# A two-layer transformer trunk in fp32r halves: plain weight units of the down projections rounded two at a time

## The reference, cut to what matters

```python
def conv_glu_ffn(h, w_up, conv_w, conv_b, w_down):
    gu = h @ w_up
    gate, up = jnp.split(gu, 2, axis=-1)
    gate = causal_depthwise_conv(gate, conv_w, conv_b)
    return (jax.nn.silu(gate) * up) @ w_down
...
        h = rms_norm(x, ffn_norm[i])
        x = x + conv_glu_ffn(h, ffn_w_up[i], ffn_conv_w[i], ffn_conv_b[i], ffn_w_down[i])
```

## Time and profile before

| | us |
|---|---|
| median of 3 runs | 2084.29 (2084.14 to 2085.8) |
| profiled execution | 2084.77 |
| its span, first to last instruction | 2083.0 |
| TensorE matmul busy | 2072.6 |
| VectorE busy | 1472.6 |
| ScalarE busy | 1069.4 |

### The profile page before, as it was taken

One profiled execution on the slowest core, in us unless ns is written; L12 is line 12 of the kernel. 1 busy time (PEld: TensorE's weight loads), 2 busy tenths in 40 slices (PEclk: granted clock), 3 DMA queues, 4 the chain that ended last, 5 costly groups with the idle time before them and its releaser, 6 DMA issues.

```text
span 2083.0 us, 30160 instructions
## 1 busy us (share of the span) xinstructions
PE 2072.6 (100%) x10836; PEld 1771.6 (85%) x10836; DVE 1472.6 (71%) x1794; ACT 1069.4 (51%) x1379; POOL 0.7 (0%) x5
## 2 busy tenths in 40 slices
PE   9999999999999999999999999999999999999999
PEld 8888888888888888888888877888888888887887
DVE  5655565567767767788986677566767767778887
ACT  6545555544444544455555566554444444445553
POOL 0000000000000000000000000000000000000000
PEclk9999999999999999999999999999999999999999
DMA  7655555656566556578776544566656666668776
GB/s 251 213 176 169 168 175 175 188 172 208 195 201 206 193 195 217 189 231 256 245 252 185 178 147 133 177 188 192 195 190 219 192 198 205 203 201 258 245 257 208
DMA packets 214043, 419.02 MB, mean 201 GB/s; under 512 B 13724, under 2 KB 18636, under 8 KB 213964
## 3 DMA queue, kind: packets, MB, share of 16 engines
q1 hardware_dynamic: 211660, 415.76, 63.3%
q10 hardware_dynamic: 2304, 2.20, 0.3%
HBM read 405.31 MB, written 12.60 MB: 201 GB/s over the span
## 4 chain that ended last, share of the span: by engine, by line
PE 94%; DVE 3%; DMA 1%; ACT 1%; issue 1%; DVEq 0%; ACTq 0%
PE ps L1341 37%; PE ps L1331 31%; PE ps L1337 16%; PE ps L1356 2%; PE ps L1358 2%; PE ps L1357 2%; DMA raw<-in_ffn_w_down 1%; PE ps L1480 1%; DVE wlo L987 0%; PE ps L1537 0%; PE ps L1548 0%; PE ps L1564 0%; PE ps L1581 0%; PE ps L1588 0%; ACT whi L696 0%
## 5 line engine op out<-in xcount | busy, mean ns | idle before, releaser
L1331 PE MATMUL ps<-hs,whi 128*128 128x512 f32 x2832 | 663.6, 390 | 0.0
L1331 PEld LDWEIGHTS ps<-hs,whi 128*128 128x128 f32 x2832 | 524.6, 188 | 104.3
L1034 DVE TENSOR_TENSOR wlo<-raw,whi 128x1024 fp32r<-128x1024 f32 x352 | 418.0, 1221 | 254.9 <-PE ps L1337 222.8
L987 DVE TENSOR_TENSOR wlo<-raw,whi 128x1024 fp32r<-128x1024 f32 x342 | 413.6, 1222 | 218.2 <-ACT whi L696 217.7
L696 ACT ACTIVATE whi<-raw 128x1024 fp32r<-128x1024 f32 x344 | 363.1, 1059 | 347.2 <-PE ps L1341 285.1
L703 ACT ACTIVATE whi<-raw 128x1024 fp32r<-128x1024 f32 x352 | 365.9, 1056 | 262.8 <-DMA raw<-in_ffn_w_up 196.9
L1337 PEld LDWEIGHTS ps<-hs,wlo 128*128 128x128 f32 x2816 | 352.6, 191 | 8.7
L1337 PE MATMUL ps<-hs,wlo 128*128 128x256 f32 x2816 | 355.3, 283 | 0.0
L1341 PE MATMUL ps<-whi,hs 128*128 128x512 f32 x1088 | 275.2, 395 | 0.7 <-ACT whi L696 0.7
L1341 PEld LDWEIGHTS ps<-whi,hs 128*128 128x128 f32 x1088 | 201.2, 188 | 41.7 <-DVE hs L1056 0.9
L1341 PE MATMUL ps<-whi,gs 128*128 128x512 f32 x864 | 214.2, 389 | 0.0
(11 more groups left out here) (190 smaller groups left out, 1559.7 us busy)
## 6 DMA issues: line engine op xcount, KB each, us to landing
raw<-in_ffn_w_up SPq DMA_DIRECT2D x352, 512.0 KB, 4.2
raw<-in_ffn_w_down SPq DMA_DIRECT2D x176, 512.0 KB, 5.2
raw<-in_fox_w_in SPq DMA_DIRECT2D x98, 512.0 KB, 3.9
raw<-in_swa_w_in SPq DMA_DIRECT2D x40, 512.0 KB, 3.7
xs<-mix SPq DMA_DIRECT2D x34, 512.0 KB, 6.0
raw<-in_fox_w_out SPq DMA_DIRECT2D x32, 512.0 KB, 3.7
raw<-in_swa_w_out SPq DMA_DIRECT2D x32, 512.0 KB, 3.7
mix<-mix_out SPq DMA_DIRECT2D x20, 512.0 KB, 6.2
```

What stands on the lines that cost most here:

```text
L987: tt(wlo[slot][:, :], raw[slot][:, :], whi[slot][:, :].bitcast(F32), ALU.subtract).then_inc(lo_ready, 1)
L1034: tt(wlo[slot][:, :], raw[slot][:, :], whi[slot][:, :].bitcast(F32), ALU.subtract).then_inc(lo_ready, 1)
L1331: return pe.matmul(ps[:, bank, :], whi[slot][:, c:c + P], moving.rearrange("p h t -> p (h t)"), start=first, stop=last)
```

## The change

Plain down units from the fifth on (place `RAW` and above in the order) are prepared in twos. At the first of two, ScalarE only waits for its landing and VectorE does nothing. At the second, ScalarE waits for that landing and for `unit_done` of the unit four before the second, and rounds both slots with one operation of 2048 columns, raising `hi_ready` by two; VectorE then makes both remainders with one operation and raises `lo_ready` by two. The buffers of `whi` and `wlo` become one tensor each, so that two neighbouring slots can be named together. SP's code, TensorE's code and the s and t units are unchanged.

```diff
-        whi = [sb(f"whi{s}", [P, UNIT], F32R) for s in range(RAW)]
-        wlo = [sb(f"wlo{s}", [P, UNIT], F32R) for s in range(RAW)]
+        whi_all = sb("whi", [P, RAW, UNIT], F32R)
+        wlo_all = sb("wlo", [P, RAW, UNIT], F32R)
+        whi = [whi_all[:, s, :] for s in range(RAW)]
+        wlo = [wlo_all[:, s, :] for s in range(RAW)]
...
+        def plain_place(u):
+
+            for layer in range(LAYERS):
+                i = u - down_unit(layer, 0)
+                if RAW <= i < 4 * DOWN_UNITS and DOWN_ORDER[layer][i][0] == "d":
+                    return i % 2
+            return None
...
             def conv_hi(u, slot):
 
+                if plain_place(u) == 0:
+                    act.wait_ge(w_land[slot], 16 * (u // RAW + 1))
+                    return
+                if plain_place(u) == 1:
+                    both = slice(slot - 1, slot + 1)
+                    act.wait_ge(w_land[slot], 16 * (u // RAW + 1))
+                    act.wait_ge(unit_done, u - RAW + 1)
+                    act.activation(whi_all[:, both, :], raw_all[:, both, :], ACT.Copy).then_inc(hi_ready, 2)
+                    return
                 act.wait_ge(w_land[slot], 16 * (u // RAW + 1))
...
                 slot = u % RAW
+                if plain_place(u) == 0:
+                    return
                 dve.wait_ge(hi_ready, u + 1)
+                if plain_place(u) == 1:
+                    both = slice(slot - 1, slot + 1)
+                    tt(wlo_all[:, both, :], raw_all[:, both, :], whi_all[:, both, :].bitcast(F32), ALU.subtract).then_inc(lo_ready, 2)
+                    return
```

## The result

| | before | after |
|---|---|---|
| median, us | 2084.22 (2083.71 to 2085.8, 4 runs) | 2134.09 (2133.34 to 2135.28, 4 runs) |
| profiled span, us | 2083.0 | 2131.5 |
| ratio of the times | | 1.0239, 95% interval 1.0227 to 1.0251 |

The change costs 49.9 us; the forecast's sum was 41.6, and 2134 lies within 2102 to 2146.

A forecast was written before the change was run, and what follows sets the result against it. TensorE, busy through the whole span, was taken as the bound, with the plain slots' loop having no slack. Terms 11.3+10.8+7.9+10.9+0.7 = 41.6 us on 2084.3 gave about 2126 us, range 2102 to 2146 (8 in 10).

The forecast's parts named there:

- What bounds the kernel: Whole span: TensorE is busy throughout, so busy time saved on ScalarE (10 us) and VectorE (7.5 us) is worth nothing.
- The ring: Plain pair's slots, mixed down order: remainders, next loads, last landing after 7.3 us, rounding, remainders; 1.46 us waiting each pass.
- steps b and c: Plain pairs: even rounding waits for the odd landing, even load issues some 1.15 us later; the loop becomes 11.66 us.
- The period: Mixed part of the down order: a plain pair's loop takes 11.66 us against TensorE's 10.20.
- Step (d): First nine s/t pairs of each layer's down projection: TensorE later by 11.3 us in layer 0, 10.8 in layer 1.
- Step (e): Second block of s/t pairs in each layer: +7.9 us in layer 0 (seven pairs), +10.9 us in layer 1 (nine).
- Step (f): Layer 0's first transposes after the last t wait longer for VectorE's fold, +0.7 us; plain stretches stay hidden.
- The sign to look for: Mixed parts: TensorE waits for `tlo` in nearly every pass, over 1 us each.
- Rival A: Plain pair's loads: time to landing is mostly queueing, so later issues land sooner; 2083 to 2087 us; 8 in 100.
- Rival B: Five transfers per cycle collide in two bursts, landing 8.2 us or more, plain stretches uncovered; 2150 or over; 12 in 100.
- Rival C: ScalarE and VectorE are late anyway in each pass; waits shrink, nothing else happens; 2082 to 2084 us; 3 in 100.
- T: The end of a plain pair's remainders, from which the loop's next issue and landings are counted.

The follow-up runs named there:

- the 12 pairs: Only the 12 plain pairs without an s/t neighbour merged, against the kernel before: 2090.88 us, ratio 1.0032.

## Why the prediction was right, and where its sizes were off

- **What bounds the kernel**: right. TensorE was full, the merged operations saved ScalarE and VectorE some busy time, and that was worth nothing.
- **The ring** (steps b and c): right in kind and nearly in size. The landing after the first issue was taken as 7.3 us and is 7.23 in the pass shown, 7.0 to 7.5 in all 32 passes that began with an empty queue. The chain of before would have hidden this ring entirely; it was found by adding up the hand-overs of one slot.
- **The period**: forecast 11.66. From the first to the ninth `tlo`, the timelines of VectorE give 1003.44 - 909.94 over eight passes, 11.69 us, in layer 0 and 1985.45 - 1890.85, 11.83 us, in layer 1. The terms that were too small are the hand-overs: to ScalarE 0.02 us was taken, and the chain has 947.46 to 947.62, 0.16 us, with two steps of its queue (L700, L701) in between; between rounding and remainders it has 0.09 where 0.02 was taken. It is made up in part by the quick issue, 0.02 where 0.1 was taken. In layer 1 single passes were longer still, up to 12.2 us.
- **Step (d)**: 24.3 us against 22.1, mostly from those passes. 0.3 us of it is a reading: the prediction took the starts of the plain units from the chain (996.98, 1955.01), and TensorE's timeline has them 0.16 us earlier (996.82, 1954.85).
- **Step (e)**: 21.9 against 18.8. In layer 1 the first `tlo` of the second block ended 25.1 us after the last t unit, as forecast (25.0). In layer 0 it ended at 26.9, because the load of unit 49 landed 7.0 us after the remainders that release it (1021.50 to 1028.51) where 5.4 had been worked out. That is no accident of one execution: the transfer itself took 6.6 us there and 4.8 in layer 1, and in the runs with remainders merged alone, with narrow operations, with the 12 pairs and with `xs` one place earlier or later it took 6.0 to 6.6 us in layer 0 and 5.0 in layer 1. Why it is slow in layer 0 isn't shown. The rest is again the passes.
- **Step (f)**: 1.6 against 0.7. TensorE waited 0.98 us at the first transposes, 0.27 before, and a few tenths at other hand-overs. The plain loops were nearly covered, as forecast; the 0.7 us at the end of layer 1 had been put at nothing.
- **The difference in all**: the steps above and the 0.7 us make 6.9 us more of span than forecast (48.5 against 41.6). The other 1.4 us are the executions: the profiled one of the kernel before is 0.6 us above its median, that of the changed kernel 0.8 below.
- **The sign to look for**: half right. TensorE does stand still in each pass, but the profile puts the first part of it down to `xs`, which lands shortly before `tlo` is made. VectorE's and TensorE's timelines in the pass of the chain above:

```profile
944.78 2.29 DVE L1010 TENSOR_TENSOR tlo<-tsum,thi 128x2048 fp32r<-128x2048 f32 x1 [0.25 <-ACT thi L713]
...
946.32 0.47 PE L1381 MATMUL ps<-whi,xs 128*128 128x512 f32 x1 [0.63 <-DMA xs<-mix]
...
947.21 0.47 PE L1381 MATMUL ps<-thi,xs 128*128 128x512 f32 x1
```

  `tlo` was finished at 944.78 + 2.29 = 947.07, and the first product behind that wait started 0.14 us later. So the wait for `xs` costs nothing here: had it landed sooner, TensorE would have stood for `tlo` all the longer.
- **Rival A** (the queueing was the ring, and later loads land sooner) fell: the queue was empty at T in every pass but the first of each second block, and three transfers still took 7.0 to 7.5 us, as the trace of before said. Yet it lay on the right axis: with the `xs` transfer out of the middle the ring fits under TensorE's 10.2 us. **Rival B** fell: the bursts did not collide; in the same passes the s and t loads had landed before the next even load went out (at 950.50 and 951.96 in the pass shown). **Rival C** fell with A.

The Trainium skill's advice on few large VectorE operations ("VectorE: DVE Perf Modes", the section on the TRN2 errata) is borne out for the busy time, 2292 ns against two of 1222, and has nothing to say about the time here. The run with all the waits and narrow operations takes as long as the changed kernel.

## What to carry to other kernels

Before two steps of a pipelined slot are merged, add up the ring of one slot: release, issue, landing of the last transfer that goes out with it, each engine's operation, hand-overs. A merge puts the first unit's work and the late release of its slot into the ring of the second, and if the ring was within a few tenths of the consumer's pace, most of that comes out in every pass (1.5 us here), although the engines that do the work are less busy. Then look at the order of the transfers: one load moved by one place in the queue was worth 40 us of the 50 in one direction and 30 in the other, where the next ring, 10.77 us, decides what is left.

## What was not expected of the hardware

- Three transfers of 512 KB into an empty queue took 7.23 us from the first issue to the last landing in the pass shown and 7.0 to 7.5 us in all 32 such passes of the changed kernel, 7.3 in the one of before. The time of a burst hardly varied once nothing else was in flight. In the kernel before, the same three behind other loads took some 9 us in one pass (first issue at 912.47, the last rounding that waited for them started at 921.57) and 7.3 in another.
- ScalarE started its merged rounding 0.16 us after a landing (947.46 to 947.62), in the run with rounding apart 0.02 us after it, and 0.07 us in the run with narrow operations, whose waits are those of the changed kernel. So the number of waits alone doesn't explain the 0.16; what does isn't shown.
